# Gated delta net inside a six-mixer stack: eight solve lanes regrouped into two waves, gate pieces and value transposes moved ahead of them

## What is computed

```
q, k, v: after a short convolution and silu; q, k normalised by their l2 norm
tri = strict_lower((kb @ k.T) * decay) + I            per chunk of 64 tokens, per head (8 heads)
u   = solve(tri, v * beta);   w = solve(tri, k * beta * exp(g))
for each of 8 chunks in order:
    v_new = u - w @ state
    o     = q_dec @ state + (q @ k.T * decay) @ v_new
    state = state * decay + k_dec.T @ v_new
y = (rms_norm(o) * gain * silu(z)) @ w_out
```

## Time and profile before

| | us |
|---|---|
| median of 3 runs | 2517.51 |
| fastest and slowest of them | 2517.42, 2524.8 |
| the profiled execution's own time | 2522.69 |
| its span, first to last instruction | 2521.0 |

### The profile page before, as it was taken

One profiled execution on the slowest core, in us unless ns is written; L12 is line 12 of the kernel. 1 busy time (PEld: TensorE's weight loads), 2 busy tenths in 40 slices (PEclk: granted clock), 3 DMA queues, 4 the chain that ended last, 5 costly groups with the idle time before them and its releaser, 6 DMA issues.

```text
span 2521.0 us, 33172 instructions
## 1 busy us (share of the span) xinstructions
PE 2379.8 (94%) x13336; PEld 1923.6 (76%) x13336; DVE 993.4 (39%) x1771; ACT 890.3 (35%) x1372; POOL 935.3 (37%) x706
## 2 busy tenths in 40 slices
PE   5999999999999979999999989999999999999996
PEld 4877787868768967877786657888888888888885
DVE  4634245235635533643314774511102354412204
ACT  3334334243433553334423443422222323322311
POOL 3333344133410013341343231644554554554542
PEclk9999999999989979999999999999999999999998
DMA  4332222023210013323222121233232333233231
GB/s 123 87 67 67 77 84 84 34 42 106 84 50 2 3 34 68 76 76 59 78 84 84 34 67 51 84 100 100 82 119 86 99 100 101 85 99 100 83 127 58
DMA packets 136738, 191.82 MB, mean 76 GB/s; under 512 B 30992, under 2 KB 84624, under 8 KB 136608
## 3 DMA queue, kind: packets, MB, share of 16 engines
q1 hardware_dynamic: 127296, 183.61, 24.8%
q10 hardware_dynamic: 9312, 6.35, 0.9%
HBM read 187.84 MB, written 2.10 MB: 75 GB/s over the span
## 4 chain that ended last, share of the span: by engine, by line
issue 63%; POOL 31%; PE 4%; DVE 1%; DMA 0%; POOLq 0%; ACT 0%; SPq 0%; ACTq 0%
POOL weights_low L644 31%; PE bank L668 1%; PE bank L670 1%; PE bank L669 1%; DMA weights_raw<-in_fox_w_in_dram 0%; POOLq L649 0%; DVE row_statistics L2248 0%; DVE x L2272 0%; DVE x L2274 0%; DVE x L2298 0%; POOLq L642 0%; ACT weights_high L1536 0%; SPq L531 0%; ACT L1536 0%; DVE row_statistics L2267 0%
## 5 line engine op out<-in xcount | busy, mean ns | idle before, releaser
L644 POOL TENSOR_TENSOR weights_low<-weights_raw,weights_high 128x512 fp32r<-128x512 f32 x688 | 932.6, 1387 | 1551.2 <-ACT weights_high L1536 1551.2
L668 PE MATMUL bank<-xt_high,weights_high 128*128 128x512 f32 (+1 forms) x1600 | 611.5, 382 | 16.8 <-POOL weights_low L644 12.7
L670 PE MATMUL bank<-xt_high,weights_low 128*128 128x512 f32 (+1 forms) x1600 | 599.4, 375 | 0.0
L669 PE MATMUL bank<-xt_low,weights_high 128*128 128x512 f32 (+1 forms) x1600 | 599.0, 374 | 0.0
L1536 ACT ACTIVATE weights_high<-weights_raw 128x2048 fp32r<-128x2048 f32 x172 | 329.0, 1914 | 685.7 <-PE bank L670 675.6
L668 PEld LDWEIGHTS bank<-xt_high,weights_high 128*128 128x128 f32 x1600 | 304.1, 190 | 86.3 <-POOL weights_low L644 24.9
L670 PEld LDWEIGHTS bank<-xt_high,weights_low 128*128 128x128 f32 x1600 | 303.3, 190 | 54.4
L669 PEld LDWEIGHTS bank<-xt_low,weights_high 128*128 128x128 f32 x1600 | 304.0, 190 | 50.0
L668 PE MATMUL bank<-weights_high,xt_high 128*128 128x512 f32 x512 | 206.4, 403 | 6.0 <-DVE xt_low L2285 2.8
L670 PE MATMUL bank<-weights_high,xt_low 128*128 128x512 f32 x512 | 200.8, 392 | 0.0
L669 PE MATMUL bank<-weights_low,xt_high 128*128 128x512 f32 x512 | 200.2, 391 | 0.0
(11 more groups left out here) (390 smaller groups left out, 2993.6 us busy)
## 6 DMA issues: line engine op xcount, KB each, us to landing
weights_raw<-in_fox_w_in_dram SPq DMA_DIRECT2D x64, 512.0 KB, 5.8
weights_raw<-in_ffn_w_gate_dram SPq DMA_DIRECT2D x44, 512.0 KB, 4.0
weights_raw<-in_ffn_w_up_dram SPq DMA_DIRECT2D x44, 512.0 KB, 4.9
weights_raw<-in_ffn_w_down_dram SPq DMA_DIRECT2D x40, 512.0 KB, 4.4
weights_raw<-in_gla_w_in_dram SPq DMA_DIRECT2D x24, 512.0 KB, 4.1
weights_raw<-in_gdn_w_in_dram SPq DMA_DIRECT2D x24, 512.0 KB, 4.5
weights_raw<-in_attn_w_qkv_dram SPq DMA_DIRECT2D x24, 512.0 KB, 4.3
weights_raw<-in_conv_w_in_dram SPq DMA_DIRECT2D x24, 512.0 KB, 4.6
```

The source lines that it names most:

```text
L644: pool.tensor_tensor(w_lo[:, odd, k], raw[:, odd, k], w_hi[:, odd, k].bitcast(F32), ALU.subtract)\
L668: pe.matmul(out_ap, lh, rh, start=first, stop=False)
L669: pe.matmul(out_ap, lh, rl, start=False, stop=False)
L670: return pe.matmul(out_ap, ll, rh, start=False, stop=last)
```

## The change

A lane's first turn is given by a new function. The two lanes of tile 0 and the two of tile 1 start at turns 0, 2, 4 and 6; those of tiles 2 and 3 start 24 turns later in the same way, at 24, 26, 28 and 30. The loop has 54 turns. The four squares of a lane come in one turn (24).

The gate parts leave the loop: pieces 5, 6 and 7 are computed whole on PE ahead of it, behind the key transposes, and ACT applies silu as it takes each of them, as for the earlier pieces.

The eight value transposes move ahead of or between the spreads: four of them around the halves of gate piece 4, where DVE scales them (`first_values`) between handing the mean squares to ACT and waiting for the roots, and four between two groups of four spreads. Keys are spread before queries. Spreads use banks 6, 7, 0, 1, keys are transposed into banks 4 and 5.

`solved_values` of a tile's first chunk moves from turn 19 to turn 20. The first batch of output norms is now 16 columns (tiles 0 and 1), the second 12, the third 4. The first batch is handled on earlier steps of the last lane, and tile 2 is normalised behind the second batch's factors.

```diff
@@ -45,8 +45,8 @@
 RECURRENCE_TURNS = (TURNS, TURNS + 1, TURNS + 2, TURNS + 3)
-SQUARE_TURNS = (TURNS + 4, TURNS + 5, TURNS + 6, TURNS + 7)
-TILE_TURNS = 12
+SQUARE_TURN = TURNS + 4
+WAVE_TURNS = TURNS + 4
@@ -73,7 +73,7 @@
-OUT_BATCHES = (slice(24), slice(24, 28), slice(28, 32))
+OUT_BATCHES = (slice(16), slice(16, 28), slice(28, 32))
@@ -95,18 +95,23 @@
+def first_turn(tt, g):
+    return WAVE_TURNS * (tt // 2) + 4 * (tt % 2) + 2 * g
...
-    for n in range((TT - 1) * TILE_TURNS + TILE_TURNS // 2 + SQUARE_TURNS[0]):
+    for n in range(first_turn(TT - 1, 1) + SQUARE_TURN):
...
             for g in range(2):
-                turn = n - tt * TILE_TURNS - g * (TILE_TURNS // 2)
-                if 0 <= turn <= SQUARE_TURNS[-1]:
+                turn = n - first_turn(tt, g)
+                if 0 <= turn <= SQUARE_TURN:
...
-GATE_PARTS = [(c, odd, k) for c in (5, 6, 7) for odd in range(2) for k in range(HALF)]
-PARTS_A_TIME = 3
+KEYS_FIRST = (4, 5, 6, 7, 0, 1, 2, 3)
+SPREAD_BANKS = (6, 7, 0, 1)
@@ -1298,15 +1303,6 @@
 norm_sums(st, list(range(8)), 8, bank[1])
-for odd in range(2):
-    gate_piece(4, odd)
-pe.wait_ge(rows_r, st["norms"] + 1)
-for n in range(8):
-    if n >= 4:
-        pe.wait_ge(gdn["qk_ready"], n - 3)
-    pe.matmul(bank[4 + n % 4][:], selector[0:8, n], scratch(st)["reciprocals"][0:8], start=True, stop=True)\
-        .then_inc(gdn["spread"], 1)
-pe.wait_ge(gdn["qk_ready"], 8)
@@ -1317,16 +1313,37 @@
-for n in range(4):
+def spread_norms(j):
+    if j >= 4:
+        pe.wait_ge(gdn["qk_ready"], j - 3)
+    pe.matmul(bank[SPREAD_BANKS[j % 4]][:], selector[0:8, KEYS_FIRST[j]], scratch(st)["reciprocals"][0:8],
+              start=True, stop=True).then_inc(gdn["spread"], 1)
+for n in range(2):
     turn_values(n)
+gate_piece(4, 0)
+for n in range(2, 4):
+    turn_values(n)
+gate_piece(4, 1)
+pe.wait_ge(rows_r, st["norms"] + 1)
+for j in range(4):
+    spread_norms(j)
+for n in range(4, 8):
+    turn_values(n)
+for j in range(4, 8):
+    spread_norms(j)
 for tt in range(TT):
-    if tt >= 2:
+    if tt < 2:
+        pe.wait_ge(gdn["values_rows"], 7 + tt)
+    else:
...
     for h in range(GDN_QK):
-        ins = pe.transpose(bank[6 + tt % 2][:, h * P:h * P + P],
+        ins = pe.transpose(bank[4 + tt % 2][:, h * P:h * P + P],
...
     ins.then_inc(gdn["keys_full"], 1)
-    turn_values(4 + tt)
+for c in (5, 6, 7):
+    for odd in range(2):
+        gate_piece(c, odd)
@@ -1475,7 +1492,6 @@
-parts = list(GATE_PARTS)
@@ -1485,16 +1501,11 @@
     solve_step(tt, g, turn - BUILD_TURNS + 1)
-if turn in (RECURRENCE_TURNS[0] - 1, RECURRENCE_TURNS[2]):
+if turn in RECURRENCE_TURNS[0::2]:
...
     (write_state if part % 2 else read_state)(2 * tt + part // 2, g)
-for c, odd, k in parts[:PARTS_A_TIME]:
-    if odd == k == 0:
-        pe.wait_ge(gdn["z_taken"], c - 1)
-    piece(st["pair"] + c // 4, c % 4, odd, bank[2 + c % 2], False, k)
-parts = parts[PARTS_A_TIME:]
@@ -2001,7 +2012,9 @@
     act.wait_ge(gdn["keys_full"], tt + 1)
-    act.activation(key_rows[:, tt], bank[6 + tt % 2][:], ACT.Copy).then_inc(gdn["keys_rows"], 1)
+    act.activation(key_rows[:, tt], bank[4 + tt % 2][:], ACT.Copy).then_inc(gdn["keys_rows"], 1)
+for n in (5, 6, 7):
+    take_gate(n)
@@ -2062,9 +2075,7 @@
-finished = [c for c, odd, k in GATE_PARTS for _ in range(odd == 1 and k == HALF - 1)]
-at_entry = [-(-GATE_PARTS.index((c, 1, HALF - 1)) // PARTS_A_TIME) for c in finished]
-for entry, (tt, g, turn) in enumerate(staggered()):
+for tt, g, turn in staggered():
@@ -2073,18 +2084,12 @@
     take_out(2 * tt + RECURRENCE_TURNS.index(turn) // 2, g)
-if turn in SQUARE_TURNS:
-    square_out(tt, g, SQUARE_TURNS.index(turn))
-if entry in at_entry:
-    c = finished[at_entry.index(entry)]
-    wait_bank(act, st, c // 4, c % 4)
-    act.activation(buf_d[:, c], bank[2 + c % 2][:], ACT.Copy).then_inc(gdn["z_taken"], 1)
-if (tt, g, turn) == (TT - 1, 1, BUILD_TURNS):
-    act.wait_ge(gdn["z_taken"], KT)
-    act.activation(buf_d[:, 5:8], buf_d[:, 5:8], ACT.Silu).then_inc(gdn["z_taken"], 1)
+if turn == SQUARE_TURN:
+    for i in range(4):
+        square_out(tt, g, i)
...
     weights_high(st["pair"] + 2, (turn - TURNS) // 2)
-if (tt, g, turn) == (TT - 1, 1, BUILD_TURNS + 13):
+if (tt, g, turn) == (TT - 1, 1, BUILD_TURNS + 2):
@@ -2122,11 +2127,13 @@
-def norm_rows(st, src, n_rows, count, eps, norm=0, base=0, n_squares=16):
+def norm_rows(st, src, n_rows, count, eps, norm=0, base=0, n_squares=16, meanwhile=None):
...
     dve.tensor_scalar(u, src[0:n_rows], 1.0 / count, eps, ALU.mult, ALU.add).then_inc(root_in, 1)
+    if meanwhile:
+        meanwhile()
@@ -2731,17 +2738,31 @@
 make_selector(gdn["selector"], GDN_V)
-norm_rows(st, bank[1], 8, 1, RMS_EPS, n_squares=8)
-for n in range(8):
-    dve.wait_ge(gdn["spread"], n + 1)
-    dve.scalar_tensor_tensor(buf_a[:, n], buf_a[:, n], float(P) ** -.5 if n < GDN_QK else 1.0,
-                             bank[4 + n % 4][:], ALU.mult, ALU.mult).then_inc(gdn["qk_ready"], 1)
-for n in range(2 * TT):
+def take_values(n):
...
         .then_inc(gdn["values_rows"], 1)
+def first_values():
+    for n in range(4):
+        take_values(n)
+def scale_keys_queries(j):
+    n = KEYS_FIRST[j]
+    dve.wait_ge(gdn["spread"], j + 1)
+    dve.scalar_tensor_tensor(buf_a[:, n], buf_a[:, n], float(P) ** -.5 if n < GDN_QK else 1.0,
+                             bank[SPREAD_BANKS[j % 4]][:], ALU.mult, ALU.mult).then_inc(gdn["qk_ready"], 1)
+norm_rows(st, bank[1], 8, 1, RMS_EPS, n_squares=8, meanwhile=first_values)
+for j in range(4):
+    scale_keys_queries(j)
+for n in range(4, 8):
+    take_values(n)
+for j in range(4, 8):
+    scale_keys_queries(j)
@@ -2834,7 +2855,7 @@
 u = out_norms[:, 0, OUT_BATCHES[k]]
-dve.wait_ge(gdn["out_squares"], (24, 28, 32)[k])
+dve.wait_ge(gdn["out_squares"], OUT_BATCHES[k].stop)
@@ -2866,20 +2887,20 @@
     if (tt, g) == (TT - 1, 1):
-        if turn == BUILD_TURNS + 12:
+        if turn == BUILD_TURNS + 2:
             out_mean(0)
-        if turn == BUILD_TURNS + 14:
+        if turn == BUILD_TURNS + 5:
...
             out_normalise(0, 0, 8)
-        if turn == RECURRENCE_TURNS[1]:
+        if turn == BUILD_TURNS + 8:
...
             out_mean(1)
-            out_normalise(2, 0, 8)
...
             out_factors(1)
-            out_normalise(3, 0, 4)
-dve.wait_ge(gdn["z_taken"], KT + 1)
+            out_normalise(2, 0, 8)
+out_normalise(3, 0, 4)
+dve.wait_ge(gdn["z_taken"], KT)
```

## The result

| | before | after |
|---|---|---|
| median of 9 runs each, same chip, us | 2518.86 | 2534.52 |
| lowest and highest of them | 2515.27, 2524.8 | 2523.68, 2542.07 |
| the profiled execution's own time | 2522.69 | 2523.68 |
| its span | 2521.0 | 2522.0 |

A forecast was written before the change was run, and what follows sets the result against it. PE's own instructions were taken to bound the kernel (busy 94% of the span). 7.5 - 12.7 + 0.9 = -4.3 us at full clock, + 3 + 6.3 for the clock = +5.0, giving 2522.5 us; range 2509 to 2536.

The forecast's parts named there:

- Ahead of the loop: Stretch before the first build: the loop starts 7.5 us later at full clock, plus 3 for the clock.
- +0.4 for the roots: Ahead of the loop: four take_values before Newton make its three steps end at 725.1 instead of 724.66.
- The clock term: Ahead of the loop: half clock during the spreads costs 3 us, bounds 0 and 6.9.
- The opening: First wave's builds: PE has 14.2 us of work, waits 15.2; all four lanes step together from 29.4 us, turn 11.
- its clock term: First wave's opening: lowered clock doubles builds, products and steps on the chain, costing 6.3 us, bounds 0 and 8.
- Rival B: Whole change: the clock holds, -4.3 us, 2513.2 us; counted against it, 44% duty in the opening; chance 0.20.
- Lockstep: Turns 11 to 19, four lanes stepping together: PE is the limit, 1.85 us a turn, 17.3 us in all.
- rival C: Clock, once down, stays down in the lockstep too: +14 us, 2531.5, up to 2540 with the second opening; chance 0.23.
- The second opening: Turns 24 to 34, second wave's builds overlapping first wave's chunks: 46.0 us for 36.5 of PE work, 9.5 waiting.
- the seven terms: Loop at full clock: 29.4 + 17.3 + 18.4 + 46.0 + 20.5 + 28.3 + 14.3 = 174.1 us, against 186.8.
- Behind it: Behind the loop: normalising tile 2 moves into the path to the first turn_out, +0.9 us.
- the fourth part: Recurrences: with both groups' chains interleaved, turns 22 to 27 and 46 to 51, PE is the limit, 8.3 us per two turns.

The follow-up runs named there:

- look1: The changed kernel run again unchanged, to catch another execution's trace: 2527.74 us.
- look2: The changed kernel run a third time unchanged, to catch another execution's trace: 2542.24 us.
- c_half: The changed kernel plus 9, 10, 12, 12 idle PE matmuls ahead of the first four lanes' products: 2535.41 us in one execution.
- c_fill: The changed kernel plus 18 to 28 idle PE matmuls ahead of each of the first four lanes' products: 2540.36 us, 1.0086 of before.

## Why the prediction was right, and where it was off

**Ahead of the loop: +11.8 instead of +10.5** (7.5, with 3 for the clock). The +0.4 for the roots did not come: N to the first spread is 8.45 against 8.44. The four take_values fit in the wait, and they push Newton's start back into the end of POOL's splits, which end at 721.37, so that the first step is quicker than before's 1.72:

```profile
721.01 0.89 DVE L2119 TENSOR_TENSOR gdn_newton<-gdn_reciprocals 8x512 f32<-8x512 f32 x1
```

The clock term was too small. From the first spread to the gate pieces the forecast had 11.4 us at full clock; the trace has 15.9 (723.40 to 739.26), so by difference 4.5 where 3 was taken. The bounds 0 and 6.9 held it here, but not in look1 and look2, where the same stretch is 3.4 us longer (7.8). Of the eight traces with the gate pieces ahead of the loop, five, these two among them, have 17.1 us of half clock there, and three have 10.3. These are the windows of after (they answer to the earlier trace rows):

```profile
723.40:728.33 4.93, 4.93 (x9) 1.68 (x9) 2.06 (x3) 0.21 (x1) 0.00 (x0) 0.73 0.45 181
728.33:732.13 3.80, 3.80 (x18) 3.00 (x17) 2.76 (x4) 0.00 (x0) 0.00 (x0) 0.50 0.00 0
732.13:735.90 3.77, 3.77 (x9) 1.54 (x9) 2.75 (x4) 0.00 (x0) 0.00 (x0) 0.95 0.00 0
735.90:739.26 3.36, 3.36 (x17) 2.99 (x17) 0.69 (x1) 1.59 (x3) 0.00 (x0) 0.50 0.00 0
739.26:755.83 16.57, 16.57 (x75) 13.46 (x74) 0.18 (x1) 1.99 (x4) 0.00 (x0) 1.00 0.00 1
```

The last row is the six gate halves at their bare price, 16.57 against the forecast's 16.3: no lane covers them. The first build comes at 755.83, in the predicted 753 to 757.

**The opening: right in kind, its clock term too large.** PE does wait in front of the products, and the longest waits of ACT are for x2 (waits of the first 34 us of the loop, total, times, longest):

```profile
ACT solve L2025 <- DVE solve L2795: 11.6, 4, 4.0
...
PE bank L1369 <- ACT solve L2026: 7.6, 4, 2.4
```

That the longest wait of PE would be 3 to 4 us before the fourth products was wrong: it is 2.4, before the first, and only 0.97 before the fourth:

```profile
759.40 0.85 PE L1369 MATMUL bank<-A 128*64 128x64 f32 x16 [2.41 <-ACT solve L2026]
764.59 1.12 PE L1369 MATMUL bank<-A 128*64 128x64 f32 x16 [2.34 <-ACT solve L2026]
...
779.53 1.12 PE L1369 MATMUL bank<-A 128*64 128x64 f32 x16 [0.97 <-ACT solve L2026]
```

The half clock makes PE's own part longer, which would shorten its waits; that is argued, no run shows it by itself. All four lanes step together from 33.3 us after S; forecast 29.4 + 6.3 = 35.7. The 29.4 was right (c_half: 29.2); the clock cost 4.1, not 6.3. (Rival B's "44% duty" does not follow from the layout, whose 14.2 us of work in 29.4 are 48%.)

**Lockstep, recurrences, end.** The lockstep runs at clock 1.00 with PE busy 22.62 of 24.00 us; rival C's "stays down" did not happen there, nor in any other trace of after. The four steps of a turn take 1.87 us (forecast 1.85), as PE's timeline of after shows from the first step of turn 12 to that of turn 13:

```profile
790.30 1.13 PE L1380 MATMUL bank<-inverse_transposed,solve 64*64 64x64 f32 x32
...
792.17 0.66 PE L1380 MATMUL bank<-cross_blocks,inverse_transposed 64*64 64x64 f32 x16
```

From ACT's first take of turn 11 to its first new_values in turn 20 it is 20.0 us. The second of these marks stands 2.2 us behind PE's start of its turn (806.9) and the first 0.7 behind it (788.42), so PE took 18.5 for the nine turns, forecast 17.3. Turns 20 to 23 took 18.0 (forecast 18.4). The recurrence's blocks have the durations of the earlier trace rows, here over the whole loop:

```profile
L2848 DVE SCALAR_TENSOR_TENSOR delta_state<-delta_state,chunk_decay,bank 128x128 f32<-128x128 f32 x56 | 19.5, 348 | 25.9 <-PE bank L1486 24.4
L1476 PE MATMUL bank<-delta_state,w_and_queries 128*128 128x128 f32 x128 | 18.5, 288 | 0.0
```

For the second wave the marks are ACT's first operation of turns 24, 35, 44 and 50 and the end of the loop. The second opening took 48.0 (forecast 46.0); half clock from 96.1 to 109.8 us after S lies in it, for which the sum had no term. Turns 35 to 43 took 19.3 (20.5), turns 44 to 49 28.0 (28.3), the end 11.9 (14.3). The loop took 178.4, in the predicted 174 to 185, 2.0 less than 174.1 + 6.3 (the seven terms add up to 174.2). Behind it, 1.16 against +0.9: the last take_out still waits behind the root's tables as in the earlier trace rows, and tile 2's rows are scaled before PE's transposes may start:

```profile
930.60 1.28 ACT L2075 ACT_TABLE_LOAD   x1
...
933.65 0.59 ACT L2058 ACTIVATE C<-bank 64x512 f32<-64x512 f32 x1
...
934.28 1.82 DVE L2869 TENSOR_TENSOR C<-C,gdn_out_norms 128x1024 f32<-128x1024 f32 x2
...
936.16 3.68 PE L893 MATMUL bank<-identity,C 128*128 128x128 f32 x16 [4.44 <-DVE C L2869]
```

The forecast of the sum, +5.0, met the profiled execution's +4.6 partly because errors cancel: +1.5 and -2.2 in the two clock terms, and in the loop, by ACT's marks, +2.7 in the lockstep (1.2 by PE's) and +2.0 in the second opening against -1.2, -0.3 and -2.4 behind it. It was luck, too, that this execution was profiled: the other two traces of after have +9.4 and +19.4.

**The median: the failed step is the fourth part.** It had "PE is the limit" in turns 22 to 27 and 46 to 51 and reckoned those turns at full clock. The second stretch kept it in the traces of after, the first did not always. PE is the limit there at either clock, and turns 25 to 28 took 21.2 us in one execution and 34.9 in another. That the median of 2534.52 us still lies in the range is owed to the range's upper part, which was made for another event: rival C had the mechanism (the clock goes down and stays down while the work is dense) and about the size (+14; +13.7 over turns 25 to 28 in look2, and the five executions of the upper group lie 10.8 to 18.4 us above the profiled one), but put it in the lockstep and tied it to the opening. c_fill and c_half show that the opening is not what triggers it. What spoke against C, that lanes in lockstep leave PE no idle time, was an argument about idleness, and the clock of this kernel does not follow idleness alone. The forecast had one row that said so (731.20 to 734.60 in the earlier trace rows) and used it only for spreads.

## What to carry to other kernels

Work that can fill an opening should stay there: the 24 gate parts cost 16.6 us bare, and with the old distance they made the loop only some 4.8 us longer as filler. When lanes are regrouped, try their distance too, and do not only count the work: four turns instead of two, with nothing else changed, made the difference between 2519.47 and 2534.52 us (1.0001 and 1.0048 of before). About 8 us of it is a shorter loop even against after's profiled execution, which has no fall at turn 25. Where a kernel's executions fall into groups, profile one of each, and compare the same turns at the same distance from a common instruction.

## What the runs showed of the hardware

The granted clock fell to half (1.2 GHz of 2.4) in stretches in which PE was busy 6.85 to 7.00 of 7.00 us and stayed there for 37.5 us (after_look2), in some executions of a kernel and not in others (in look1 for 6.8 us at the same place, in the profiled after not there). The Trainium skill (TensorE: Matmul & The Clock Gate, Part 1) says that the clock follows how busy PE has been and that sustained activity releases the throttle. The traces agree in c_half's opening, where filling the waits held the clock at 1.00 with PE busy 27.01 of 29.30 us, where after had 0.60 with 22.30 of 30.20. They do not agree in look2's turns 25 to 28, where full PE lost the clock, nor ahead of the loop, where transposes that kept PE busy 3.80 of 3.80 us ran at 0.50.

DVE's first Newton step, an 8x512 product, took 0.89 us in after and 1.72 in before, with POOL splitting weights beside the first 0.4 us of the one and the first 1.2 us of the other; the two steps behind it take 0.68 in either. That POOL's work is the cause is not tested by a run of its own.
